# Hybrid decoder trunk on one core: the DeltaNet's q and k are no longer normalised, and their norms are applied elsewhere

## The reference

```python
def l2_normalize(t):
    tf = t.astype(jnp.float32)
    return tf * lax.rsqrt(jnp.sum(tf * tf, axis=-1, keepdims=True) + EPS)

def gated_deltanet(q, k, v, z, b, a, conv_w, a_log, dt_bias, norm_w):
    qkv = jax.nn.silu(causal_depthwise_conv(jnp.concatenate([q, k, v], axis=-1), conv_w))
    q, k, v = jnp.split(qkv, 3, axis=-1)
    q = l2_normalize(q.reshape(B, S, DN_HEADS, DN_HEAD_DIM)) * (DN_HEAD_DIM ** -0.5)
    k = l2_normalize(k.reshape(B, S, DN_HEADS, DN_HEAD_DIM))
    beta = jax.nn.sigmoid(b)
    g = -jnp.exp(a_log) * jax.nn.softplus(a + dt_bias)
    o = chunk_gated_delta_rule(q, k, v, g, beta)      # needs k k^T, q k^T, a triangular inverse
    o = rms_norm(o, norm_w) * jax.nn.silu(z)
```

## Time and profile before

| | |
|---|---|
| time, median of 3 runs | 1039.43 us (1039.07 to 1040.08) |
| the profiled execution's own time | 1039.46 us |
| its span in the profile | 1037.6 us |
| TensorE busy | 1022.0 us, 98% of the span |
| VectorE, ScalarE, GpSimd busy | 71%, 58%, 21% |
| share of the chain that ended last | TensorE 94% |

### The profile page before, as it was taken

How to read it: one execution, slowest core, us unless ns; L and a number is a source line. 1 busy time by engine, 2 the same in 40 slices (tenths; PEclk the granted TensorE clock), 3 DMA queues, 4 the chain that set the end, 5 groups by cost and what they waited for, 6 DMA issues and landing times.

```text
span 1037.6 us, 18950 instructions
## 1 busy us (share of the span) xinstructions
PE 1022.0 (98%) x6474; PEld 887.8 (86%) x6474; DVE 739.7 (71%) x1202; ACT 606.6 (58%) x1069; POOL 219.8 (21%) x254
## 2 busy tenths in 40 slices
PE   9999999999999999999999999999999999999996
PEld 7888888898988788888878888889989888888885
DVE  6677666799776766666676666678986867666665
ACT  6555555777556555555665555558775556555554
POOL 2866111100400321111122111110014013111111
PEclk9999999999999999999999999999999999999998
DMA  7966666584124566666647666665822238666651
GB/s 248 280 198 185 196 189 180 142 253 134 63 63 122 179 207 186 193 187 183 203 126 218 183 183 191 193 175 150 229 97 66 88 97 252 191 183 193 190 183 40
DMA packets 249881, 176.79 MB, mean 170 GB/s; under 512 B 5875, under 2 KB 235400, under 8 KB 249704
## 3 DMA queue, kind: packets, MB, share of 16 engines
q1 hardware_dynamic: 248800, 174.35, 56.6%
q0 software_dynamic: 400, 1.43, 0.5%
q10 hardware_dynamic: 632, 0.34, 0.1%
HBM read 175.05 MB, written 1.05 MB: 170 GB/s over the span
## 4 chain that ended last, share of the span: by engine, by line
PE 94%; DVE 2%; ACT 2%; POOL 1%; issue 0%; DVEq 0%; POOLq 0%; ACTq 0%
PE bank L746 29%; PE bank L751 15%; PE bank L730 13%; PE bank L731 13%; PE bank L732 13%; PE bank L792 1%; PE bank L1128 1%; PE bank L1141 1%; PE bank L799 1%; PE bank L757 1%; PE bank L1061 1%; PE bank L1014 1%; DVE X L1899 0%; DVE Wl L1857 0%; POOL gact L616 0%
## 5 line engine op out<-in xcount | busy, mean ns | idle before, releaser
L1857 DVE TENSOR_TENSOR Wl<-raw,Wh 128x1024 fp32r<-128x1024 f32 x324 | 416.9, 1295 | 78.0 <-ACT Wh L1393 77.9
L1393 ACT ACTIVATE Wh<-raw 128x1024 fp32r<-128x1024 f32 x323 | 330.5, 1053 | 80.0 <-PE bank L732 78.1
L746 PE MATMUL bank<-X,Wh 128*128 128x512 f32 x1344 | 336.5, 392 | 0.0
L746 PEld LDWEIGHTS bank<-X,Wh 128*128 128x128 f32 x1344 | 246.7, 188 | 48.9
L616 POOL TENSOR_TENSOR gact<-gact,pooled 128x256 f32<-128x256 f32 x88 | 81.3, 924 | 569.9 <-DVE gact L1956 422.7
L751 PEld LDWEIGHTS bank<-X,Wl 128*128 128x128 f32 x1344 | 182.5, 189 | 14.7 <-DVE Wl L1857 1.2
L751 PE MATMUL bank<-X,Wl 128*128 128x256 f32 x1344 | 187.7, 282 | 0.0
L730 PE MATMUL bank<-Wh,aH 128*128 128x512 f32 x336 | 132.7, 395 | 4.9 <-DVE aL L1977 4.9
L731 PE MATMUL bank<-Wl,aH 128*128 128x512 f32 x336 | 131.8, 392 | 0.0
L732 PE MATMUL bank<-Wh,aL 128*128 128x512 f32 x336 | 131.5, 391 | 0.0
L1508 ACT ACTIVATE dec<-bank 128x256 f32<-128x256 f32 x88 | 33.7, 383 | 117.3 <-PE bank L751 117.3
(11 more groups left out here) (314 smaller groups left out, 1295.0 us busy)
## 6 DMA issues: line engine op xcount, KB each, us to landing
raw<-in_ffn_w_gate SPq DMA_DIRECT2D x88, 512.0 KB, 3.8
raw<-in_ffn_w_up SPq DMA_DIRECT2D x88, 512.0 KB, 3.7
raw<-in_ffn_w_down SPq DMA_DIRECT2D x88, 512.0 KB, 4.4
raw<-in_w_in SPq DMA_DIRECT2D x48, 512.0 KB, 4.3
raw<-in_w_out SPq DMA_DIRECT2D x16, 512.0 KB, 3.3
cst<-in_consts POOLq DMA_DIRECT2D x1, 1200.0 KB, 6.3
xr<-in_x SPq DMA_DIRECT2D x2, 512.0 KB, 4.1
out_x<-big SPq DMA_DIRECT2D x3, 256.0 KB, 2.7
```

The costliest lines, as they stand in the source:

```text
L746: nc.tensor.matmul(b[:, :], piece(Wh, s)[:, k, :], X[:, k, :, :], start=k == 0, stop=False)
L1393: return nc.scalar.activation(Wh[:, s, 0:D_MODEL], raw[:, s, :], ACT.Copy).then_inc(hi_cast.sem, 1)
L1857: return nc.vector.tensor_tensor(Wl[:, s, 0:D_MODEL], raw[:, s, :], Wh[:, s, 0:D_MODEL].bitcast(F32), ALU.subtract).then_inc(lo_cast.sem, 1)
```

## The change

q and k stay as the convolution and SiLU leave them. The sums of squares are taken with the squares as the stationary operand and one column of ones as the moving one: four products per head (q and k, two halves), each 128 x 128 by 128 x 1, into one column of bank 3 each. So the sums stand with positions on the partitions, where `ga` has its columns. DVE adds epsilon to k's sums, makes epsilon times q's sums for the output norm, inverts k's sums and multiplies beta with them (`beta_k`). ACT makes the square root by Ln and Exp on eight columns, and multiplies `V` with it, unit by unit, two units after each level's copy.

```diff
-        gstep = signal("gstep", 15)
+        gstep = signal("gstep", 19)
...
                 def sum_squares(h):
                     pe.wait_ge(*squared.at(layer, h + 1))
-                    pe.wait_ge(*convd.at(layer, 4 + h))
-                    nc.tensor.matmul(bank[3 + h][:, :], ones, sq[:, h % 3, :], start=True,
-                                     stop=True).then_inc(sumsq.sem, 1)
+                    pe.wait_ge(*convd.at(layer, 4))
+                    for a in range(2):
+                        for c in range(HALVES):
+                            at = (1 - a) * UNITS + 4 * c + h
+                            m = nc.tensor.matmul(bank[3][:, at:at + 1], sq[:, h % 3, a * SEQ + c * P:a * SEQ + (c + 1) * P],
+                                                 ones[:, 0:1], start=True, stop=True)
+                    m.then_inc(sumsq.sem, 1)
...
                 def z_piece(h):
                     split(POS_Z + h)
-                    pe.wait_ge(*ln2.at(layer, 2 + h))
+                    pe.wait_ge(*convd.at(layer, 5 + h))
...
-                pe.wait_ge(*ln2.at(layer, 1))
+                pe.wait_ge(*gstep.at(layer, 17))
                 for c in range(HALVES):
                     nc.tensor.matmul(bank[2 + c][:, :], ones, grow[:, 4 * c:4 * c + 4, :], start=True,
...
                     if n == 0:
-                        pe.wait_ge(*normed.at(layer, 4))
-                        pe.wait_ge(*ln2.at(layer, 4))
+                        pe.wait_ge(*conv_act.at(layer, 8))
...
                 pe.wait_ge(*pm_done.at(layer, 2 * N_LEVELS))
+                pe.wait_ge(*normed.at(layer, 2))
...
-                for h in range(DN_HEADS):
-                    log_norm(h)
-                    inverse_norm(h)
-                    if h == 0:
-                        hi_mix(layer, 21)
-                    if h == 1:
-                        conv_first(10)
-                    if h == 2:
-                        hi_mix(layer, 22)
+                hi_mix(layer, 21)
+                conv_first(10)
+                hi_mix(layer, 22)
+                act.wait_ge(*gstep.at(layer, 16))
+                nc.scalar.activation(ga[:, 5, 8:16], ga[:, 4, 8:16], ACT.Ln).then_inc(k_log.sem, 1)
+                act.wait_ge(*k_log.at(layer, 1))
+                nc.scalar.activation(ga[:, 7, 8:16], ga[:, 5, 8:16], ACT.Exp, scale=0.5).then_inc(k_norm.sem, 1)
                 conv_first(11)
                 hi_mix(layer, 23)
...
                         nc.scalar.activation(even, src, ACT.Copy).then_inc(d_done.sem, 1)
+                    act.wait_ge(*k_norm.at(layer, 1))
+                    act.wait_ge(*v_copied.at(layer, n // 2 + 1))
+                    for u in (2 * n, 2 * n + 1):
+                        op = nc.scalar.activation(V[:, u, :], V[:, u, :], ACT.Copy, scale=ga[:, 7, 8 + u:9 + u])
+                    op.then_inc(normed.sem, 1)
...
+                dve.wait_ge(*sumsq.at(layer, 4))
+                small(nc.vector.tensor_scalar(k_sq, bank[3][:, 0:UNITS], EPS, None, ALU.add))
+                small(nc.vector.tensor_scalar(q_eps, bank[3][:, UNITS:2 * UNITS], EPS, EPS / DN_SCALE ** 2, ALU.add, ALU.mult))
+                small(nc.vector.reciprocal(k_inv, k_sq))
+                small(nc.vector.tensor_tensor(beta_k, beta, k_inv, ALU.mult))
                 lo_mix(layer, 21)
-                l2norm(0)
-                l2norm(1)
                 conv_rest(10)
-                l2norm(2)
-                l2norm(3)
                 conv_rest(11)
```

More of the change, by code:

```diff
@@ L224, in build @@
         sq = early[:, 0:1536].rearrange("p (b t) -> p b t", b=3)
-        inv = early[:, 1536:2560].rearrange("p (b t) -> p b t", b=2)
-        def inv_of(h):
-            return inv[:, h, :] if h < 2 else sq[:, h - 1, :]
         V = early[:, 0:1024].rearrange("p (u d) -> p u d", u=UNITS)
@@ L375, in build @@
         sumsq = signal("sumsq", 4)
-        ln2 = signal("ln2", 4)
-        inv_done = signal("inv_done", 4)
+        k_log = signal("k_log", 1)
+        k_norm = signal("k_norm", 1)
         normed = signal("normed", 4)
@@ L1602, in square @@
                                          ACT.Square).then_inc(squared.sem, 1)
[L1604 to L1611, removed]
                 def z_silu(h):
@@ L1710, in mixer @@
                     act.wait_ge(*v_turned.at(layer, c + 1))
-                    act.wait_ge(*normed.at(layer, 4))
                     nc.scalar.activation(V[:, 4 * c:4 * c + 4, :].rearrange("p u d -> p (u d)"), bank[6 + c][:, :],
@@ L2169, in mixer @@
                 small(nc.vector.scalar_tensor_tensor(row(9), row(1), -1.0, per_head(19), ALU.mult, ALU.mult))
-                beta, gc, eg, neg_e = ga[:, 7, :], ga[:, 16, :], ga[:, 17, :], ga[:, 18, :]
-                lo_mix(layer, 21)
[L2173 to L2177, removed]
-                l2norm(0)
-                l2norm(1)
+                beta, gc, eg, neg_e = ga[:, 7, 0:8], ga[:, 16, :], ga[:, 17, :], ga[:, 18, :]
+                k_sq, k_inv, beta_k, q_eps = ga[:, 4, 8:16], ga[:, 6, 8:16], ga[:, 8, 8:16], ga[:, 11, 8:16]
+                dve.wait_ge(*sumsq.at(layer, 4))
[3 more added lines that the diff above has]
+                small(nc.vector.tensor_tensor(beta_k, beta, k_inv, ALU.mult))
+                lo_mix(layer, 21)
                 conv_rest(10)
-                l2norm(2)
-                l2norm(3)
                 conv_rest(11)
@@ L2205, in unit_gram @@
                         u = 2 * n + j
-                        op = nc.vector.scalar_tensor_tensor(LT[:, u, :], b[:, j, 1, :], beta[:, u:u + 1], dec[:, u, :],
+                        op = nc.vector.scalar_tensor_tensor(LT[:, u, :], b[:, j, 1, :], beta_k[:, u:u + 1], dec[:, u, :],
                                                             ALU.mult, ALU.mult)
@@ L2267, in new_values @@
                     nc.vector.tensor_tensor(Vn[:, u, :], bank[(4, 7)[c]][:, :].rearrange("p (u d) -> p u d", u=4),
-                                            beta[:, u].unsqueeze(2).broadcast_to([P, 4, P]), ALU.mult).then_inc(vn_done.sem, 1)
+                                            beta_k[:, u].unsqueeze(2).broadcast_to([P, 4, P]), ALU.mult).then_inc(vn_done.sem, 1)
                 def mask_scores(h):
@@ L2293, in out_variance @@
                     dve.wait_ge(*o_ss.at(layer, c + 1))
-                    nc.vector.tensor_scalar(ost[:, c, 1, :], ost[:, c, 0, :], 1.0 / P, EPS, ALU.mult,
-                                            ALU.add).then_inc(o_var.sem, 1)
+                    nc.vector.scalar_tensor_tensor(ost[:, c, 1, :], ost[:, c, 0, :], 1.0 / P, q_eps[:, 4 * c:4 * c + 4], ALU.mult,
+                                                   ALU.add).then_inc(o_var.sem, 1)
                 def out_norm(c):
@@ L2321, in mixer @@
                 dve.wait_ge(*neg_eg.at(layer, 1))
+                dve.wait_ge(*normed.at(layer, 4))
                 for h in range(DN_HEADS):
```

## The result

The changed kernel takes 1042.95 us (median of 16 executions, 1040.64 to 1043.98), against 1040.03 for the kernel before in the same comparison. The ratio is 1.0027, with a 95% interval of 1.002 to 1.0034: slower, by some 2.9 us or 0.3%. The forecast was 1039.8 us and no change, with a range up to 1040.9. It was wrong.

What follows compares the result with a forecast made beforehand. The prediction took TensorE, busy 98% of the span, as the bound. The profiled 1039.46 us plus 0.3 us of longer sums in both layers, all else hidden, gave 1039.8 us, range 1038.6 to 1040.9.

Steps and rivals of the forecast that it cites:

- The stream of the sums: TensorE's 32 one-column passes a layer at 0.112 us: 3.58 us added, 3.43 removed, so 0.15 us more a layer.
- The 25 ns floor: Skill rule for products of up to 64 columns; by it alone the 64 passes take 1.6 us, a gain of 5.3.
- The first two rivals: Passes of the sums cheap: 1036.2 or 1034.4 us, chance 0.07; or dear at 0.19 us each: 1044.8 us, chance 0.04.
- the third rival: TensorE's clock falls to 1.2 GHz, doubling v piece 2 behind the sums: 5.7 us in two layers, 1045.5 us, chance 0.03.
- the signs that the prediction named as speaking against it: Load distance under 0.074 or over 0.14 us, clock below 1.00 at 244 to 252 us, TensorE waiting for `ga`, `D` or `early`.
- ScalarE: Two scalings behind each level's copies, 0.56 us, fit in ACT's waits of 1.66 and 1.60 us for TensorE; no cost.
- VectorE: Four small operations, 0.85 us, replace 2.7 us per layer; DVE waits 0.7 us for the sum of head 3; no cost.
- The Gram's consumer: L2206 on DVE already waited 1.05 us for TensorE, so it cannot start earlier: no gain, no loss.
- the removed norm was hidden: In each mixer the normalising is already hidden behind TensorE, so removing it gains nothing; the rival against this had 0.02.

Runs made afterwards that it cites:

- the last two experiments: The kernel before with four 512-column fp32r sums a layer, norm kept: 1036.26 us; the changed kernel with those sums, not brought to the partitions: 1034.66 us.
- the last run: The changed kernel with four 512-column fp32r sums a layer, leaving out the step that brings them to the partitions: 1034.66 us against 1039.57, ratio 0.9952.

## Why the prediction was wrong

**The stream of the sums was right.** A one-column fp32 pass with a 128 x 128 weight costs its load: predicted 0.112 us, measured 0.112 between loads, and 0.14 us more a layer in the chain where 0.15 was the sum. The rule of the Trainium skill that stood by it ("TensorE: Matmul & The Clock Gate", "LDWEIGHTS (loading the stationary operand)") says 107 ns for 128 columns; these rows agree, with 2.57 us for 24 passes in the chain, 0.107 each. The 25 ns floor of its section "Back-to-back issue gap" is not what bounds such a pass. The first two rivals, cheap and dear passes, are out.

**What failed is the clock.** The sum had no term for it: it took a granted clock of 1.00 through the sums and v piece 2, and the third rival, which said otherwise, was weighed at almost nothing. The prediction named the place, v piece 2 behind the stretch, and the mechanism, a fall from 2.4 to 1.2 GHz in a stretch in which next to nothing streams, but gave it 0.03. It leaned on the window from 280 to 290 us, where small passes leave the clock whole. Those passes have 32 or 64 columns under narrow loads, and between them stand projections with 256 columns every 0.12 us. They are no likeness of 24 passes with one column. The runs with 8, 16 and 32 columns in a row of 24, and those with one column in rows of 8 and 16, show that both the few columns and the length of the row count. The trace of before had no stretch of this kind, so the case should have been a real part of the range: with it at 0.2 or more, the upper end would have been near its 1045.5. Its size was also too high: 5.7 us, because all of v piece 2 was doubled in both layers. Measured are 1.53 us a layer, 3.1 for both in the profiled execution, and 2.6 by the medians (1042.95 against the 1040.28 to 1040.35 of the three kernels with 32 such passes and a whole clock). The half speed covers only a part of the piece (it begins 0.9 us into it in layer 1), and passes of 256 columns go from 0.12 to 0.21 us, not to 0.24. Of the signs that the prediction named as speaking against it, this one came: windows at 248 to 252 us with a clock below 1.00.

**ScalarE.** Its scalings took 0.39 us each, 0.68 for two instead of 0.56. Its timeline in the last two levels:

```profile
280.54 0.68 ACT L1712 ACTIVATE early<-early,ga 128x128 f32<-128x128 f32 x2
281.24 1.28 ACT L1717 ACT_TABLE_LOAD   x1
283.60 0.28 ACT L1708 ACTIVATE D<-bank 128x128 f32<-128x128 f32 x1 [1.08 <-PE bank L1138]
...
284.24 0.68 ACT L1712 ACTIVATE early<-early,ga 128x128 f32<-128x128 f32 x2
284.83 1.05 ACT L1391 ACTIVATE Wh<-raw 128x1024 fp32r<-128x1024 f32 x1
286.90 0.52 ACT L1726 ACTIVATE D<-bank 32x128 f32<-32x128 f32 x2 [1.02 <-PE bank L1162]
```

ACT waited for TensorE 1.66 and 1.60 us before, and waits 1.08 and 1.02 now: the scalings came out of idle time, as forecast. **VectorE** waited 2.31 us for the sum of head 3, not 0.7, since the half clock delayed it: with 32 columns and the clock whole the same wait is 0.81 us. The Gram's consumer still waits for TensorE, 2.27 us instead of 1.05:

```profile
252.63 0.17 DVE L2164 TENSOR_SCALAR ga<-bank 128x8 f32<-128x8 f32 x1 [2.31 <-PE bank L1011]
...
264.03 0.61 DVE L2193 SCALAR_TENSOR_TENSOR four<-bank,ga,dec 128x128 f32<-128x128 f32 x2 [2.27 <-PE bank L1058]
```

That the removed norm was hidden is right for this kernel, and the last two experiments show how near it was to the path: with TensorE 2.6 us a layer ahead (3.43 less 0.86), it is on it.

## What to carry to other kernels

On a bound TensorE, ask of each pass whether its load or its columns set its price. Here a pass with a new 128 x 128 weight took 0.10 to 0.11 us with 1 to 128 columns, and one of 512 columns 0.43 us in fp32 and 0.23 in fp32r. So eight passes of 512 fp32 columns and 32 of one column took the same time. What made the sums shorter was fewer loads and passes, by fp32r (2.9 us, with the norm applied elsewhere), or the wide product in fp32r (3.7 us, with the norm as it was). The 4.9 us of the last run are a bound, since the step that it leaves out has a price that no run here gives.

Look out for many near-empty passes in a row. In these runs the fall was gone with 32 columns of ones, which were free under the load, or with the passes spread in groups of eight. Look at the granted clock in windows of 2 us, since a slice of the page is too long to show a fall.

## What the runs showed of the hardware that was not expected

- 24 fp32 passes of one column in a row, 2.6 us at 100% busy TensorE, were followed by a fall of the clock from 2.4 to 1.2 GHz; the windows of 2 us behind them show 0.54 and 0.61. In the five falls behind such a row that have a trace it began between a little before the end of the row (16 columns) and 1.4 us behind it. It was whole again from 252 us on, with passes of 256 columns running all the while.
- With the same passes and loads, the fall came with 1, 8 and in part with 16 columns, and in none of 11 executions each with 32 or 128. 16 passes of one column in a row, 1.68 us, did not bring it in 11 executions.
- Whether it falls differs from one execution of a kernel to the next: 13 of 16 with one column; with 16 columns 6 of 11, one of these in one layer only (by the mean clock; windows for the profiled executions).
- In a row of short fp32 passes a weight load of 128 x 128 starts every 0.112 us with 1, 8, 32 and 128 columns alike (24 loads in 2.76 us each time).
- With three passes of 512 columns in fp32r instead, one execution of five shows a fall (windows of 0.61 and 0.53 from 270 us on) behind 2 us in which TensorE was busy for 1.41.
